# A hybrid decoder layer on one core: the second norm's root is spread by a transposition and two transfers, and DVE's scans, convolutions and a Strassen product stand in another order

## The chip, the cores and the metric

The kernel runs on one core of a Trainium2 chip. Its time is the device time of one execution in microseconds; the median of the runs is given. Engines are named as the profile names them: PE is TensorE, DVE is VectorE, ACT is ScalarE, POOL is GpSimd and SP is SyncE, which here issues transfers only.

## What is computed

One decoder layer over 512 tokens of width 1024, in float32:

```
x = x + 0.5 * swiglu(rmsnorm(x, ffn1_norm), gate, up, down)      # FF 2816
h = rmsnorm(x, mix_norm)
proj = h @ w_in                    # q, k, v, o, gates, pool channels
qk = silu(causal_dwconv(proj[q, k], conv_w, conv_b))             # 4 taps
hm = mlstm_chunkwise(q, k, v, i_pre, f_pre)                      # 4 heads x 128
hm = sigmoid(o) * (hm * rsqrt(mean(hm * hm) + EPS) * mh_norm)
hp = multiscale_pool(proj[pool], pool_w, pool_scale)
x = x + concat(hm, hp) @ w_out
x = x + 0.5 * swiglu(rmsnorm(x, ffn2_norm), gate, up, down)
return rmsnorm(x, final_norm)
```

where `rmsnorm(x, g) = x * rsqrt(mean(x * x) + EPS) * g`, the mean going over the 1024 channels of a token.

## The kernel before, in words

**Layout.** x lies with channels on the 128 partitions and the 512 tokens along the free axis (`x[P, 8, T]`). Every product is made in three passes of reduced-precision matmuls (`three_passes`, L412 to L416): high times high, high times low, low times high. So each weight unit of 128x1024 that SP loads into `raw` (two buffers, L297) is split by ACT into `w_hi` (L845) and by DVE into `w_lo` (L1309); four slots hold split units. The norm's gain goes into x before the product, and the root, one number a token, is multiplied into the product afterwards, by DVE, from `rinv[P, T]`, the same row on every partition.

**Order.** Nothing schedules this program: each engine's list of instructions is written out by hand in its own function, and semaphores join them. The stages are the first FFN (`ffn_up`, `ffn_down`), the mixer, the second FFN and the last norm.

**A norm's root.** While the squares are being summed over partitions, PE makes four columns of means (`mean_columns`, L473, one column for each block of 128 tokens). DVE turns them into roots in ten dependent steps on a [128, 4] tile (`inverse_rms`, L1354, and `rsqrt`, L1339 to L1347), each counted in `col_step`. Then `replicate` (L477) has PE spread them: for each of the four blocks one fp32 matmul of 128x128 with the column broadcast as the stationary operand and the identity as the moving one (L465) gives the row on all partitions of PSUM bank 7. DVE copies that to `rinv` (`take_rinv`, L1363). The kernel does so for the first, second and third norm.

**The mixer's first part.** Units are numbered from MIX. Unit MIX holds the gates. Then come units MIX+1, 2, 3, 4, 6, 7, 9, 10 (`QK_UNIT`, one block of q or k each, 8 k-steps of three matmuls into one of three PSUM banks in turn), MIX+5, 8, 11, 12 (`V_UNIT`), and from MIX+13 (`O_UNIT`) on the output gates and pool channels. PE runs the second norm's means inside the first q/k block (`mean_hook`) and `replicate(1)` right behind that block. From the fourth q/k block on it waits until DVE has read the bank three blocks back (`u_made`).

On DVE, `mixer` begins with the root (`inverse_rms(1)`), `take_rinv(1)`, `gates_in` (the gates' product with rinv at L1629, two small operations, L1631 and L1632) and a split. Then each round of the loop over units reads the block's product, times rinv, into `work` (L1682), runs the three taps of the convolution for the block before (`taps`, L1661), splits a unit, and makes the low half of the finished q/k (`qk_lo`, L1672). `gates_first` and `gates_second` (scans at L1647, L1651, L1653) stand in the rounds of `V_UNIT[0]` and `V_UNIT[1]`. ACT starts the gates' logarithm after DVE's product (L1067 to L1071) and the convolution's first tap (L1089).

**The heads' roots.** Each head's root is spread in another way: PE transposes the [128, 4] columns to 4 rows of 128 (`head_turn`, L691), ACT copies them to `turned` (L1150), SP writes them to DRAM (L381) and, when that has landed, reads them back onto all partitions (`spread_root`, L385), and DVE multiplies by them (L1748).

**The Strassen loops.** All but a few of the 22 gate/up blocks of an FFN are made by a scheme of seven products on halves (`period`, L519 to L521: 84 matmuls of 256 columns, in the order 1, 5, 3 of the iteration before, 6, 4 of the iteration before, 2, 7). The first matmul of a period waits for `prod_made`, DVE's product of silu and up of two iterations before (`product`, L1460 and L1462). DVE's `iteration` holds four sums of weight blocks (L1399, L1407, L1411, L1418), seven low halves (L1426), the gate (L1451, L1454), the product and two corners (L1468, L1474). SP reloads each of the four weight blocks when DVE has used it (L315). Iterations 0 and 1 are written out, the others stand in a loop.

## Time and profile before

| what | value |
|---|---|
| median of 3 runs | 895.78 us (895.74 to 896.03) |
| the profiled execution | 896.22 us, span in the profile 894.4 us |
| PE busy | 887.2 us (99%), 5572 matmuls |
| PE weight loads | 804.4 us (90%) |
| DVE busy | 673.8 us (75%), 1158 instructions |
| ACT busy | 450.1 us (50%) |
| POOL busy | 42.7 us (5%) |
| chain that ended last | PE 95%, DVE 3%, ACT 1% |
| granted clock of PE, mean | 0.998 of full speed |
| DVE busy, 120 to 270 us | 124.41 of 150 us |
| DVE busy, 50 to 120 us | 67.11 of 70 us |
| DVE busy, 360 to 420 us | 44.08 of 60 us |

The span goes from the first to the last instruction; the device time is a little longer. Matmuls overlap and their ends are modelled, so PE's busy time says little of short stalls: the distance between the starts of two matmuls says more. The first Strassen loop lies at about 52 to 227 us, the mixer begins at about 353 us, and the second loop at about 562 us. Line numbers are those of the kernel before.

### The profile page before, as it was taken

How to read it: one execution, taken by the hardware profiler on the slowest of the kernel's cores; microseconds unless marked ns; L12 is line 12 of the kernel's file. 1: busy time of each engine (PE TensorE's matmuls, PEld its weight loads, DVE VectorE, ACT ScalarE, POOL GpSimd, SP SyncE). 2: the span in 40 equal slices, each digit the busy share in tenths (PEclk: the TensorE clock that was granted, in tenths of full speed). 3: DMA queues.
4: the chain of work that ended last, by engine and by line, in shares of the span. 5: the costliest groups of instructions: out<-in, count | busy, mean ns of one | idle time of the engine just before them, and what ended most of it. 6: DMA issues, size and time to landing. Idle time of an engine off the chain costs nothing.

```text
span 894.4 us, 15568 instructions
## 1 busy us (share of the span) xinstructions
PE 887.2 (99%) x5572; PEld 804.4 (90%) x5572; DVE 673.8 (75%) x1158; ACT 450.1 (50%) x753; POOL 42.7 (5%) x63
## 2 busy tenths in 40 slices
PE   9999999999999999999999999999999999999997
PEld 7899999999988888888888888999999999888887
DVE  7999999999553534677886699899999998534334
ACT  7665666666432323444853374666666665323221
POOL 0000000000000000001435100000000000000000
PEclk9999999999999999999999999999999999999999
DMA  6233333332523332223323232333323332433312
GB/s 247 94 116 98 97 112 104 110 94 70 177 104 108 100 111 95 93 72 107 107 72 99 83 125 71 107 106 111 100 95 111 100 114 84 136 113 99 112 48 95
DMA packets 39420, 93.84 MB, mean 105 GB/s; under 512 B 4436, under 2 KB 5092, under 8 KB 39384
## 3 DMA queue, kind: packets, MB, share of 16 engines
q1 hardware_dynamic: 39064, 92.83, 31.7%
q0 software_dynamic: 176, 0.46, 0.2%
q8 instruction: 22, 0.36, 0.2%
q14 instruction: 14, 0.11, 0.0%
q10 hardware_dynamic: 144, 0.08, 0.0%
HBM read 91.24 MB, written 2.11 MB: 104 GB/s over the span
## 4 chain that ended last, share of the span: by engine, by line
PE 95%; DVE 3%; ACT 1%; issue 1%; DMA 0%; DVEq 0%; SPq 0%; ACTq 0%
PE ps L414 16%; PE ps L416 16%; PE ps L415 16%; PE ps L519 14%; PE ps L521 14%; PE ps L520 13%; PE ps L444 1%; PE ps L447 1%; PE ps L450 1%; DVE w_lo L1426 1%; PE ps L465 0%; PE ps L820 0%; PE ps L674 0%; PE ps L682 0%; DMA raw<-weights 0%
## 5 line engine op out<-in xcount | busy, mean ns | idle before, releaser
L1309 DVE TENSOR_TENSOR w_lo<-raw,w_hi 128x1024 fp32r<-128x1024 f32 x83 | 101.6, 1224 | 118.7 <-ACT w_hi L845 112.9
L414 PE MATMUL ps<-act_hi,w_hi 128*128 128x512 f32 (+1 forms) x470 | 178.7, 380 | 0.0
L416 PE MATMUL ps<-act_hi,w_lo 128*128 128x512 f32 (+1 forms) x470 | 178.2, 379 | 0.0
L415 PE MATMUL ps<-act_lo,w_hi 128*128 128x512 f32 (+1 forms) x470 | 178.2, 379 | 0.0
L519 PE MATMUL ps<-xg_hi,w_hi 128*128 128x256 f32 x608 | 174.1, 286 | 0.3 <-DVE work L1462 0.3
L521 PE MATMUL ps<-xg_hi,w_lo 128*128 128x256 f32 x608 | 172.2, 283 | 0.0
L520 PE MATMUL ps<-xg_lo,w_hi 128*128 128x256 f32 x608 | 171.9, 283 | 0.0
L845 ACT ACTIVATE w_hi<-raw 128x1024 fp32r<-128x1024 f32 x75 | 79.0, 1056 | 150.9 <-PE ps L416 146.0
L519 PE MATMUL ps<-xe_hi,w_hi 128*128 128x256 f32 x456 | 128.0, 281 | 0.0
L521 PE MATMUL ps<-xe_hi,w_lo 128*128 128x256 f32 x456 | 127.2, 279 | 0.0
L520 PE MATMUL ps<-xe_lo,w_hi 128*128 128x256 f32 x456 | 127.2, 279 | 0.0
L519 PEld LDWEIGHTS ps<-xg_hi,w_hi 128*128 128x128 f32 x608 | 116.2, 191 | 1.8 <-issue 0.9
L520 PEld LDWEIGHTS ps<-xg_lo,w_hi 128*128 128x128 f32 x608 | 116.1, 191 | 0.1
L521 PEld LDWEIGHTS ps<-xg_hi,w_lo 128*128 128x128 f32 x608 | 116.1, 191 | 0.0
L897 ACT ACTIVATE w_hi<-sums 128x512 fp32r<-128x512 f32 x152 | 94.5, 626 | 21.2 <-DVE sums L1399 15.5
L416 PEld LDWEIGHTS ps<-act_hi,w_lo 128*128 128x128 f32 x470 | 88.4, 188 | 16.8
L415 PEld LDWEIGHTS ps<-act_lo,w_hi 128*128 128x128 f32 x470 | 88.4, 188 | 16.6
L414 PEld LDWEIGHTS ps<-act_hi,w_hi 128*128 128x128 f32 x470 | 88.4, 188 | 16.3
L1426 DVE TENSOR_TENSOR w_lo<-sums,w_hi 128x512 fp32r<-128x512 f32 x152 | 100.9, 683 | 1.3 <-ACT w_hi L897 1.3
L519 PEld LDWEIGHTS ps<-xe_hi,w_hi 128*128 128x128 f32 x456 | 85.9, 188 | 0.1
L520 PEld LDWEIGHTS ps<-xe_lo,w_hi 128*128 128x128 f32 x456 | 85.7, 188 | 0.0
L521 PEld LDWEIGHTS ps<-xe_hi,w_lo 128*128 128x128 f32 x456 | 85.6, 188 | 0.0
(221 smaller groups left out, 1377.9 us busy)
## 6 DMA issues: line engine op xcount, KB each, us to landing
raw<-weights SPq DMA_DIRECT2D x85, 512.0 KB, 3.3
raw<-weights SPq DMA_DIRECT2D x152, 256.0 KB, 2.7
x<-x_t SPq DMA_DIRECT2D x8, 256.0 KB, 6.0
first<-weights SPq DMA_DIRECT2D x8, 256.0 KB, 5.7
work<-neg_rows SPq DMA_DIRECT2D x4, 256.0 KB, 3.2
root<-root_rows SPq DMA_DIRECT2D x4, 256.0 KB, 3.8
out<-sums SPq DMA_DIRECT2D x3, 256.0 KB, 2.1
out<-raw SPq DMA_DIRECT2D x3, 256.0 KB, 2.2
```

What stands on the lines that cost most here:

```text
L414: pe.matmul(acc, hi, m_hi, start=first, stop=False)
L415: pe.matmul(acc, hi, m_lo, start=False, stop=False)
L416: return pe.matmul(acc, lo, m_hi, start=False, stop=last)
L444: pe.matmul(ps[:, n], weight(n, k)[0], plain_x(k, 0), start=k == 0, stop=False)
L447: pe.matmul(ps[:, n], weight(n, k)[1], plain_x(k, 0), start=False, stop=False)
L519: pe.matmul(acc, hi[:, at], m_hi, start=first and k == 0, stop=False, skip_group_check=True)
L520: pe.matmul(acc, hi[:, at], m_lo, start=False, stop=False, skip_group_check=True)
L521: mm = pe.matmul(acc, lo[:, at], m_hi, start=False, stop=k == KH - 1, skip_group_check=True)
L845: act.activation(w_hi[:, k % SLOTS], raw[:, k % RAWS], ACT.Copy).then_inc(hi_made, 1)
L897: act.activation(factor(i, par, p)[0], src, ACT.Copy).then_inc(f_hi[i], 1)
L1309: dve.tensor_tensor(w_lo[:, k % SLOTS], raw[:, k % RAWS], f32(w_hi[:, k % SLOTS]), ALU.subtract).then_inc(lo_made, 1)
L1426: dve.tensor_tensor(lo, src, f32(hi), ALU.subtract).then_inc(f_lo[i], 1)
```

## The change

It does three things.

1. The second norm's root is no longer spread by `replicate(1)` and `take_rinv(1)`. PE transposes the columns once (`turn_norm`), before the last k of the first q/k block instead of behind the block. ACT copies the four rows to `turned` (`turn_norm_out`, ahead of its gate operations), SP writes them to a new DRAM tensor `norm_rows` and reads them back into `rinv` on all partitions (`spread_norm`, between the loads of units MIX+5 and MIX+6). DVE waits for that (`norm_spread`) just before the gates' product. The other norms keep the old way.
2. DVE's order in the mixer: the split of unit MIX+4 comes before the gates' product; `gates_second` comes before the split and the low half of its round; the last q/k block is scaled, and the taps of the one before it are run, before the split of unit MIX+13; the last taps come before the copy of the gate columns, and the last low half before the split of unit MIX+14.
3. In iteration 1 of both Strassen loops DVE makes `product` before `sum_4`.

```diff
@@ SP
+            def spread_norm(i):
+                sp.wait_ge(norm_turned, i + 1)
+                sp.dma_start(norm_rows[i].rearrange("(b p) -> b p", p=P),
+                             (turned, mask)[i][0:TB]).then_inc(norm_out, 16)
+                sp.wait_ge(norm_out, 16 * (i + 1))
+                sp.dma_start(rinv[:], norm_rows[i:i + 1].partition_broadcast(P)).then_inc(norm_in, 16)
...
-            units(DN1 + RAWS, MIX + 15)
+            units(DN1 + RAWS, MIX + 6)
+            spread_norm(0)
+            units(MIX + 6, MIX + 15)
@@ PE
+            def turn_norm(stage):
+                pe.wait_ge(col_step, STEPS * (stage + 1))
+                pe.transpose(ps[0:TB, 7, 0:P], ycol[:], ident[:]).then_inc(rep_made, 1)
...
                 def mean_hook(k):
                     if k == 2:
                         mean_columns(1)
+                    if k == KD - 1:
+                        turn_norm(1)
...
                         column_block(n, n, ps[:, qk_bank[i % 3]], mean_hook if i == 0 else None)
-                        if i == 0:
-                            replicate(1)
@@ ACT
+            def turn_norm_out(i):
+                act.wait_ge(rep_made, i + 2)
+                if i >= 1:
+                    act.wait_ge(root_out, 16 * HEADS)
+                act.activation((turned, mask)[i][0:TB], ps[0:TB, 7, 0:P], ACT.Copy).then_inc(norm_turned, 1)
...
                 act.preload_act_table_set("natural_log_exp_and_others")
+                turn_norm_out(0)
@@ DVE
+            def norm_spread(i):
+                dve.wait_ge(norm_in, 16 * (i + 1))
...
                     if not tail:
                         lo_of(6, s + 1, 1 - par)
+                    if second:
+                        product(s - 1, 1 - par)
+                    if not tail:
                         sum_4(s + 1)
-                    if not head:
+                    if not head and not second:
                         product(s - 1, 1 - par)
...
-                iteration(1, 1)
+                iteration(1, 1, second=True)
...
                 inverse_rms(1)
-                take_rinv(1)
...
+                    split_next()
                     dve.wait_ge(g_sum, 2)
+                    norm_spread(0)
                     dve.tensor_tensor(arena[0:36, 0], arena[0:36, 1], rinv[0:36, :], ALU.mult).then_inc(g_dve, 1)
...
+                def scaled(i):
+                    dve.wait_ge(unit_used, QK_UNIT[i] + 1)
+                    dve.tensor_tensor(work[:, i % 2], ps[:, qk_bank[i % 3]], rinv[:], ALU.mult).then_inc(u_made, 1)
...
                 gates_in()
-                split_next()
                 pending = None
                 for n in range(MIX + 1, V_UNIT[2]):
-                    if n in QK_UNIT:
+                    if n in QK_UNIT and n < QK_UNIT[7]:
                         i = QK_UNIT.index(n)
-                        dve.wait_ge(unit_used, n + 1)
-                        dve.tensor_tensor(work[:, i % 2], ps[:, qk_bank[i % 3]], rinv[:], ALU.mult).then_inc(u_made, 1)
+                        scaled(i)
                     if pending is not None:
                         taps(pending)
+                    if n == V_UNIT[1]:
+                        gates_second()
+                    if n == QK_UNIT[6]:
+                        scaled(7)
+                        taps(6)
                     if n < QK_UNIT[7]:
                         split_next()
                         if pending is not None:
                             qk_lo(pending)
-                    pending = i if n in QK_UNIT else None
+                    pending = i if n in QK_UNIT and n < QK_UNIT[6] else None
                     if n == V_UNIT[0]:
                         gates_first()
-                    if n == V_UNIT[1]:
-                        gates_second()
+                taps(7)
                 dve.wait_ge(cols_made, 1)
                 dve.tensor_copy(cols[:], ps[:, 3, 0:2 * TB * HEADS]).then_inc(cols_made, 1)
-                taps(7)
                 qk_lo(6)
+                qk_lo(7)
                 split_next()
-                qk_lo(7)
```

How the instructions stand in the built programs, at the three places that matter. Line numbers are each program's own.

DVE at the start of the mixer, from the root's last step to the first q/k scaling; before, then changed:

```order
L1347 SCALAR_TENSOR_TENSOR ycol<-bcol,ycol 128x4 [waits col_step]
L1359 COPY rcol<-ycol 128x4 [waits col_step]
L1363 COPY rinv<-ps 128x512 [waits rep_made]
L1625 COPY arena<-ps 36x512 [waits rinv_made]
L1627 TENSOR_TENSOR arena<-ps,arena 36x512 [waits g_sum]
L1629 TENSOR_TENSOR arena<-arena,rinv 36x512 [waits g_sum]
L1631 TENSOR_SCALAR arena<-arena,vec 4x512 [waits g_dve]
L1632 TENSOR_SCALAR arena<-arena,vec 4x512
L1309 TENSOR_TENSOR w_lo<-raw,w_hi 128x1024 [waits hi_made]
L1682 TENSOR_TENSOR work<-ps,rinv 128x512 [waits unit_used]
```

```order
L1373 SCALAR_TENSOR_TENSOR ycol<-bcol,ycol 128x4 [waits col_step]
L1385 COPY rcol<-ycol 128x4 [waits col_step]
L1656 COPY arena<-ps 36x512
L1658 TENSOR_TENSOR arena<-ps,arena 36x512 [waits g_sum]
L1335 TENSOR_TENSOR w_lo<-raw,w_hi 128x1024 [waits hi_made]
L1662 TENSOR_TENSOR arena<-arena,rinv 36x512 [waits norm_in,g_sum]
L1664 TENSOR_SCALAR arena<-arena,vec 4x512 [waits g_dve]
L1665 TENSOR_SCALAR arena<-arena,vec 4x512
L1704 TENSOR_TENSOR work<-ps,rinv 128x512 [waits unit_used]
```

The copy of rinv is gone, the split of unit MIX+4 has moved from behind the gates' operations to ahead of them, and the gates' product now waits for the transfer (`norm_in`).

DVE at the sixth to eighth q/k block (i = 5, 6, 7): from the taps of block 5 to the low halves of blocks 6 and 7; before, then changed:

```order
L1661 SCALAR_TENSOR_TENSOR work<-work,vec 128x509 [waits conv_step]
L1309 TENSOR_TENSOR w_lo<-raw,w_hi 128x1024 [waits hi_made]
L1672 SCALAR_TENSOR_TENSOR act_lo<-work,act_hi 128x512 [waits qk_hi_made]
L1651 SCALAR_TENSOR_TENSOR arena<-arena 4x512
L1652 TENSOR_SCALAR sums<-arena 4x512 [waits g_dve]
L1653 SCALAR_TENSOR_TENSOR arena<-arena 4x512
L1682 TENSOR_TENSOR work<-ps,rinv 128x512 [waits unit_used]
L1309 TENSOR_TENSOR w_lo<-raw,w_hi 128x1024 [waits hi_made]
L1682 TENSOR_TENSOR work<-ps,rinv 128x512 [waits unit_used]
L1661 SCALAR_TENSOR_TENSOR work<-work,vec 128x511 [waits conv0,u_made]
```

```order
L1694 SCALAR_TENSOR_TENSOR work<-work,vec 128x509 [waits conv_step]
L1684 SCALAR_TENSOR_TENSOR arena<-arena 4x512
L1685 TENSOR_SCALAR sums<-arena 4x512 [waits g_dve]
L1686 SCALAR_TENSOR_TENSOR arena<-arena 4x512
L1335 TENSOR_TENSOR w_lo<-raw,w_hi 128x1024 [waits hi_made]
L1709 SCALAR_TENSOR_TENSOR act_lo<-work,act_hi 128x512 [waits qk_hi_made]
L1704 TENSOR_TENSOR work<-ps,rinv 128x512 [waits unit_used] x2
L1694 SCALAR_TENSOR_TENSOR work<-work,vec 128x511 [waits conv0,u_made]
L1694 SCALAR_TENSOR_TENSOR work<-work,vec 128x510 [waits conv_step]
L1694 SCALAR_TENSOR_TENSOR work<-work,vec 128x509 [waits conv_step]
L1335 TENSOR_TENSOR w_lo<-raw,w_hi 128x1024 [waits hi_made]
```

The scans pass a split and a low half; the last split of each piece, that of unit MIX+13, now stands behind both scalings and the three taps.

DVE in iteration 1 of a Strassen loop, around the product; before, then changed:

```order
L1426 TENSOR_TENSOR w_lo<-sums,w_hi 128x512 [waits f_hi6]
L1418 TENSOR_TENSOR sums<-raw,sums 128x512 [waits f_lo3,s2_made,blk_in1]
L1460 TENSOR_TENSOR work<-work 128x256 [waits c22_made,silu_made]
L1462 TENSOR_TENSOR work<-ps,work 128x256 [waits p_done4]
L1426 TENSOR_TENSOR w_lo<-raw,w_hi 128x512 [waits f_hi4]
```

```order
L1455 TENSOR_TENSOR w_lo<-sums,w_hi 128x512 [waits f_hi6]
L1489 TENSOR_TENSOR work<-work 128x256 [waits c22_made,silu_made]
L1491 TENSOR_TENSOR work<-ps,work 128x256 [waits p_done4]
L1447 TENSOR_TENSOR sums<-raw,sums 128x512 [waits f_lo3,s2_made,blk_in1]
L1455 TENSOR_TENSOR w_lo<-raw,w_hi 128x512 [waits f_hi4]
```

The sum has moved behind the two multiplications; what follows keeps its place.

## Rows read from the trace of the kernel before

**Rows 1.** The waits of TensorE: engine, line, waited for, us in total, times, longest.
```profile
PE ps L820 <- DVE sums L1893: 1.2, 1, 1.2
PE ps L519 <- DVE work L1462: 0.3, 1, 0.3
```

**Rows 2.** Timeline, TensorE, second norm's broadcasts: start, us, engine, line, instruction, count.
```profile
363.40 0.39 PE L416 MATMUL ps<-xg_hi,w_lo 128*128 128x512 f32 x1
363.62 1.05 PE L465 MATMUL ps<-ident,ycol 128*128 128x128 f32 x8
...
364.98 0.39 PE L416 MATMUL ps<-xg_hi,w_lo 128*128 128x512 f32 x1
```

**Rows 3.** Timeline, TensorE, a transposition of the same form for head 3.
```profile
476.30 0.39 PE L416 MATMUL ps<-xg_hi,w_lo 128*128 128x512 f32 x1
476.52 0.27 PE L691 MATMUL ps<-ident,ycol 128*4 128x128 f32 x1
...
477.10 0.39 PE L416 MATMUL ps<-xg_hi,w_lo 128*128 128x512 f32 x1
```

**Rows 4.** Timeline, all engines, head 0's root: transposition, second issue, DVE's reader.
```profile
448.35 0.27 PE L691 MATMUL ps<-ident,ycol 128*4 128x128 f32 x1
...
450.12 0.32 SPq L385 DMA_DIRECT2D root<-root_rows  x1
...
454.24 0.69 DVE L1748 TENSOR_TENSOR arena<-arena,root 128x512 f32<-128x512 f32 x1 [0.45 <-DMA root<-root_rows]
```

**Rows 5.** Timeline, DVE in the mixer.
```profile
361.38 0.16 DVE L1347 SCALAR_TENSOR_TENSOR ycol<-bcol,ycol 128x4 f32<-128x4 f32 x1
...
366.88 0.68 DVE L1629 TENSOR_TENSOR arena<-arena,rinv 36x512 f32<-36x512 f32 x1
...
368.51 1.21 DVE L1309 TENSOR_TENSOR w_lo<-raw,w_hi 128x1024 fp32r<-128x1024 f32 x1
369.64 0.67 DVE L1682 TENSOR_TENSOR work<-ps,rinv 128x512 f32<-128x512 f32 x1
...
418.53 1.23 DVE L1309 TENSOR_TENSOR w_lo<-raw,w_hi 128x1024 fp32r<-128x1024 f32 x1 [1.83 <-ACT w_hi L845]
...
420.27 2.73 DVE L1661 SCALAR_TENSOR_TENSOR work<-work,vec 128x511 f32<-128x511 f32 x3
```

**Rows 6.** Timeline, TensorE: first matmuls of units MIX+4 and MIX+13.
```profile
375.43 0.39 PE L414 MATMUL ps<-xg_hi,w_hi 128*128 128x512 f32 x1
...
427.05 0.44 PE L414 MATMUL ps<-xg_hi,w_hi 128*128 128x512 f32 x1
```

**Rows 7.** Timeline, TensorE, first Strassen loop, iterations 1 to 3.
```profile
68.69 0.28 PE L521 MATMUL ps<-xe_hi,w_lo 128*128 128x256 f32 x1
...
69.51 0.28 PE L520 MATMUL ps<-xg_lo,w_hi 128*128 128x256 f32 x1
...
79.28 0.28 PE L521 MATMUL ps<-xe_hi,w_lo 128*128 128x256 f32 x1
79.42 0.38 PE L519 MATMUL ps<-xg_hi,w_hi 128*128 128x256 f32 x1
```

**Rows 8.** Timeline, DVE, the same iterations.
```profile
67.80 0.68 DVE L1418 TENSOR_TENSOR sums<-raw,sums 128x512 f32<-128x512 f32 x1
68.40 0.41 DVE L1460 TENSOR_TENSOR work<-work 128x256 f32<-128x256 f32 x1
...
72.59 0.69 DVE L1399 TENSOR_TENSOR sums<-raw 128x512 f32<-128x512 f32 x1 [0.37 <-DMA raw<-weights]
...
78.87 0.42 DVE L1462 TENSOR_TENSOR work<-ps,work 128x256 f32<-128x256 f32 x1
```

**Rows 9.** Timeline, ACT, the silu of iteration 1.
```profile
66.71 0.63 ACT L901 ACTIVATE work<-work 128x512 f32<-128x512 f32 x1 [1.07 <-DVE work L1454]
```

**Rows 10.** Waits of all engines, one row.
```profile
DVE sums L1399 <- DMA raw<-weights: 8.7, 32, 0.8
```

**Rows 11.** DMA issues by line: engine, count, KB each, median us to landing.
```profile
x<-x_t SPq DMA_DIRECT2D x8, 256.0 KB, 6.0
```

More of the change, by code:

```diff
@@ L105, with build_layer @@
 S_COLS = 1280
-def build_layer(nc, weights, pool_w, x_t, vecs, consts, neg_rows, root_rows, out):
+def build_layer(nc, weights, pool_w, x_t, vecs, consts, neg_rows, root_rows, norm_rows, out):
     ctx = ExitStack()
@@ L239, in build_layer @@
         half_made, qsq_made = sem("half_made"), sem("qsq_made")
+        norm_turned, norm_out, norm_in = sem("norm_turned"), sem("norm_out"), sem("norm_in")
         turn_made, root_out, root_in = sem("turn_made"), sem("root_out"), [sem(f"root_in{i}") for i in range(2)]
@@ L551, in period @@
                     if head:
-                        pe.wait_ge(rinv_made, stage + 1)
+                        pe.wait_ge(rinv_made, 1 + p)
                     else:
@@ L1149, in turn_out @@
                         act.wait_ge(root_out, 16 * h)
+                    else:
+                        act.wait_ge(norm_out, 16)
                     act.activation(turned[0:TB], ps[0:TB, 7, 0:P], ACT.Copy).then_inc(turn_made, 1)
@@ L1363, in take_rinv @@
                 dve.tensor_copy(rinv[:], ps_rep).then_inc(rinv_made, 1)
-                dve.wait_ge(rinv_made, stage + 1)
+                dve.wait_ge(rinv_made, 1 + stage // 2)
             def terms(p, k):
@@ L1474, in corner_22, with iteration @@
                     dve.tensor_tensor(u_half[1], ps_b[par], p5_sb[par], ALU.add).then_inc(c22_made, 1)
-                def iteration(s, par, head=False, tail=False):
+                def iteration(s, par, head=False, tail=False, second=False):
                     if not tail:
@@ L1992 @@
     root_rows = nc.dram_tensor("root_rows", (HEADS, T), F32, kind="Internal").ap()
-    build_layer(nc, *args, neg_rows, root_rows, out)
+    norm_rows = nc.dram_tensor("norm_rows", (2, T), F32, kind="Internal").ap()
+    build_layer(nc, *args, neg_rows, root_rows, norm_rows, out)
     r = run_bass_kernel_spmd(nc, [arrays], core_ids=[0])
```

## The prediction

> **What bounds the kernel now.** I read the waits of TensorE first, since a change to a vector-side detail is worth what it takes out of the engine that sets the end. The profile lists three, of which two count: 1.2 us at the very start and 0.3 us before L519 on DVE's L1462 [rows 1]. So the time is TensorE's own instruction stream, and I weigh it by the distance between starts of matmuls (the ends are modelled). Then come the stretches that the change touches: TensorE around the four broadcasts of the second norm [rows 2] and around an isolated transposition of the same form [rows 3], the existing pair of root transfers [rows 4], DVE and TensorE in the mixer [rows 5, 6], and the two engines in the Strassen loop [rows 7, 8]. The reader is to see that in the mixer TensorE waits for nobody, while in the loop DVE is just as full as TensorE.
>
> **Part 1, the second norm.** Four fp32 matmuls of L465 go, one transposition comes.
> - Removed: L416 starts at 363.40, the four broadcasts follow, and the third matmul behind them (L416) starts at 364.98: 1.58 us for three steps [rows 2]. A step of this stream is 0.227 us: from this L416 to the first matmul of the fourth q/k block at 375.43 are 46 steps and 10.45 us [rows 2, 6], and three steps are 0.68. Cost 1.58 - 0.68 = 0.90 us.
> - Added: the same reading around head 3's transposition: 476.30 to 477.10 is 0.80 us for three steps [rows 3], so it costs 0.80 - 0.68 = 0.12 us.
> - Net: 0.90 - 0.12 = 0.78 us less TensorE time, on the path, since nothing in the mixer holds TensorE back.
>
> By its duration in the row the transposition is 0.27 us [rows 3], and that is the other bound of its cost; I take 0.12, because the path pays the distance between starts and the end of a matmul is only modelled. The Trainium skill (TensorE: Matmul & The Clock Gate, Part 4) gives about 275 ns for one in a kernel's context; by that figure the estimate of the saving would be 0.62 us in place of 0.78. The duration of the row agrees with it, the distance between starts does not.
>
> Does the transposition wait? It stands before the last k of its block, two steps before 363.40, so at 362.94. DVE's last step of the root starts at 361.38 and takes 0.16 [rows 5]. It is ready 1.4 us earlier: no wait.
>
> What it starts is longer than before: copy on ACT, a 2 KB transfer out, a 256 KB broadcast in. Head 0's root does just this: transposition at 448.35, second issue at 450.12, DVE's reader at 454.24, 5.89 us in all [rows 4]. From 362.94 that gives 368.8 for DVE's gate product (L1629), which ran at 366.88 [rows 5]. From L1629 to the next split are 1.63 us (366.88 to 368.51) and the first scaling (L1682) takes 0.67 [rows 5], so that scaling ends at 368.8 + 1.6 + 0.7 = 371.1, 0.8 us later than before. DVE fills the wait: the copy of rinv is gone, and the 1.2 us split of unit MIX+4, 368.51 before, comes ahead of it. Who waits? TensorE's fourth q/k block (unit MIX+4) needs this scaling for its bank. It began at 375.43 [rows 6] and would now begin at 374.65. Cover: 3.5 us. Behind the waiting DVE product stand the scaling and the split of unit MIX+5, and that unit is not read before the block after, 5.4 us later. ACT's three gate operations move by the same 2 us and are ahead of nothing that TensorE needs sooner. On SP the load of unit MIX+6 now stands behind both transfers, but it could never start before the split of MIX+4, which was at 368.51: with the split moved ahead it starts earlier, not later. Cost 0.
>
> **Part 2, scans, convolutions, splits in the mixer.** Same instructions, other order. The scans and the row of negatives come sooner, by at least the split and the low half that they pass: TensorE was not waiting for them, gain 0. The one thing made later is the split of unit MIX+13: it ran at 418.53 and now stands behind a scaling (0.7) and the three taps (2.7) [rows 5], so by the worst count it starts at 421.9 and ends at 423.2. TensorE reads it at 427.05, or 426.3 after the saving [rows 6]. Cost 0; without that 3 us cover it would be a direct stall.
>
> **Part 3, the first product in each Strassen loop.** In iteration 1 the two multiplications L1460 and L1462 now precede the sum L1418, which takes DVE 0.60 us (67.80 to 68.40) [rows 8]. In the first FFN this is where the 0.3 us wait of [rows 1] sits: from 68.69 to the second start behind it, 69.51, are 0.82 us, where two steps of 0.119 (69.51 to 79.28, 82 steps) would be 0.24 [rows 7]. So 0.58 us are lost, and L1462 0.60 us sooner would remove nearly all of it. Nothing stops the swap: ACT's silu started at 66.71 and takes 0.63 [rows 9], so it is done before DVE would reach L1460 at 67.80 [rows 8]; and the TensorE product that L1462 reads is the fifth of the seven of a period, the seventh being under way by then.
>
> But is it kept? TensorE's next period starts at 79.42 [rows 7], again just behind L1462 (78.87 + 0.42 = 79.29) [rows 8]. Between the two DVE is idle once, 0.37 us at 72.59, for a transfer [rows 8], and that transfer is released by DVE's own L1426 behind the product, which keeps its time: the swap only permutes three instructions in front of it. The same idle, and no other, stands in the later iterations: 32 waits, 8.7 us [rows 10]. So DVE's chain runs on its own clock, TensorE would arrive at 79.42 - 0.58, wait, and go on at 79.42. Bounds: 0 and 0.58 us; I take 0, since 79.42 is fixed by DVE. In the second FFN [rows 1] shows no such wait, and 0 is the only value.
>
> **Sum.** -0.78 + 0 + 0 = -0.78 us. The profiled execution took 896.22 us (span 894.4) and would take 895.44; it lay 0.44 above the median of the three runs, 895.78, so the median becomes **895.0 us**. That is 0.09%, and a measurement of this kernel tells about 0.2% (1.8 us) from no change.
>
> **Rivals.**
> - *The product's gain is kept too.* For it: the wait is real and is removed. Against: the start at 79.42 is again 0.13 us behind L1462. It gives 895.78 - 0.78 - 0.58 = 894.4.
> - *The saved matmuls are given back.* TensorE, 0.78 us ahead, would then run into something that keeps its time, as in part 3. In the mixer no wait is listed [rows 1], and the second loop starts from work that TensorE itself releases, so it moves along. It gives 895.8.
> - *The transfers come late (the slower side).* The only known pair lands in time, but a transfer in a full queue can take 6.0 us, as those of x at the start do [rows 11]. If both took that, the gate product would begin 12.0 us behind the transposition and more, in place of 5.9 [rows 4], so 6.1 later; the cover is 3.5, and TensorE would stand still for 2.6 us before the fourth q/k block: 895.0 + 2.6 = 897.6. It decides from 3.5 us of delay. Against: the queue holds no other load there, since MIX+5 was issued before and MIX+6 comes behind.
> - *More than the sum.* Some wait within DVE's chain shortens in every iteration. It would need over 1.8 us in total; nothing in the rows says so. 893.8 or less.
>
> **Numbers.** Forecast 0.76; product's gain kept 0.10; given back 0.06; transfers late 0.04; more than the sum 0.04. The range runs from 894.2 (the kept gain, less 0.2 for the spread of runs) to 896.0 (given back, with the same spread). Faster by over 0.2%: 0.04, and 0.01 for errors of mine in the same direction, 0.05. Slower by over 0.2%: the late transfers, 0.05 with the same. Within: 0.90.
>
> **What would show it.** One transposition before the last k of the first q/k block and no stall around it; three steps across it of about 0.80 us; DVE's gate product at about 368.8 and idle before it, put down to a transfer; TensorE without a wait at the fourth q/k block; L1460 in the first loop at 67.8 in place of 68.40, TensorE's period there starting at 68.8, and the next one still at 79.4 with a listed wait where there was none. If the next one starts at 78.9, part 3 is wrong. If TensorE shows a wait on L1682's scaling, part 1 is. A time outside 894.2 to 896.0 means a mechanism that I have not seen.

## The result and the profile after

The changed kernel takes **897.35 us** (median of 21 runs, 896.11 to 898.46) against 895.92 us (21 runs, 894.97 to 896.59) for the kernel before beside it: a ratio of 1.0016, 95% interval 1.0010 to 1.0022. The forecast was 895.0 us in a range of 894.2 to 896.0: the change loses 1.4 us (0.9 to 2.0 by the interval) where 0.8 were to be gained. The profiled execution took 897.64 us (span 895.8), 1.42 us more than the one of before, so the loss is in the trace.

First the timeline of all engines around the second norm, the part of the change that was to gain (columns as in [rows 2]; weight loads and the plain matmuls in between left out):

```profile
363.05 0.27 PE L496 MATMUL ps<-ident,ycol 128*4 128x128 f32 x1
363.19 1.21 DVE L1335 TENSOR_TENSOR w_lo<-raw,w_hi 128x1024 fp32r<-128x1024 f32 x1
363.36 0.27 ACT L1076 ACTIVATE turned<-ps 4x128 f32<-4x128 f32 x1 [3.41 <-PE ps L496]
363.65 0.33 SPq L356 DMA_DIRECT2D norm_rows<-turned  x1
364.84 0.35 SPq L359 DMA_DIRECT2D rinv<-norm_rows  x1
365.54 0.34 SPq L298 DMA_DIRECT2D raw<-weights  x1
368.94 0.68 DVE L1662 TENSOR_TENSOR arena<-arena,rinv 36x512 f32<-36x512 f32 x1 [4.54 <-DMA rinv<-norm_rows]
```

All as forecast. The transposition waits for nothing, the split of MIX+4 fills DVE's wait, and the gates' product starts at 368.94 (forecast 368.8, [rows 5] 366.88). Two of the matmuls around it:

```profile
362.82 0.39 PE L427 MATMUL ps<-xg_hi,w_lo 128*128 128x512 f32 x1
...
363.62 0.39 PE L427 MATMUL ps<-xg_hi,w_lo 128*128 128x512 f32 x1
```

Three steps across the transposition take 0.80 us, where the four broadcasts made them 1.58 [rows 2]: 0.78 us are saved. So where does 1.42 come from? I set milestones on TensorE side by side: the first of the mean's matmuls in each stage, and the first and last matmul of each Strassen loop.

| stretch on TensorE | before | after |
|---|---|---|
| first loop, first to last matmul | 182.01 us | 182.79 us |
| mixer, second norm's mean to third norm's mean | 358.61 to 545.04 | 358.71 to 544.94 |
| second loop, first to last matmul | 561.86 to 762.95 (201.09) | 561.78 to 764.37 (202.59) |

The first loop began 0.68 us earlier and ended at the same time (233.53, 233.63). The mixer is 0.2 us shorter; its 0.78 are there, but 0.6 of them are lost again at head 0. The **second loop is 1.50 us longer**, and that is the loss. No part of the change touches that loop by more than one permutation in its second iteration. TensorE's first matmul of it and DVE at its head, of before:

```profile
561.86 0.28 PE L519 MATMUL ps<-xg_hi,w_hi 128*128 128x256 f32 x1
...
563.51 0.69 DVE L1432 TENSOR_TENSOR act_lo<-work,act_hi 128x512 fp32r<-128x512 f32 x1 [0.70 <-ACT act_hi L906]
564.21 0.69 DVE L1399 TENSOR_TENSOR sums<-raw 128x512 f32<-128x512 f32 x1
```

and of after:

```profile
561.78 0.28 PE L535 MATMUL ps<-xg_hi,w_hi 128*128 128x256 f32 x1
...
563.43 0.69 DVE L1461 TENSOR_TENSOR act_lo<-work,act_hi 128x512 fp32r<-128x512 f32 x1 [0.70 <-ACT act_hi L922]
565.07 0.69 DVE L1428 TENSOR_TENSOR sums<-raw 128x512 f32<-128x512 f32 x1 [0.95 <-DMA raw<-weights]
```

DVE's first sum over weight blocks starts 0.86 us later (3.29 us behind TensorE's first matmul of the loop, and not 2.35), for a transfer that it did not wait for before. SP issued it at the same place (561.50 before, 561.42 after). What is in its way shows in the DMA queues of two stretches. Before, 560.4 to 561.4 us, ahead of the blocks:

```profile
q8 instruction: 1, 0.02, 5.9%
```

Before, 562.1 to 564.7 us, while the blocks come:

```profile
q1 hardware_dynamic: 288, 0.52, 62.4%
issues: line engine op xcount, KB each, median us to landing
raw<-weights SPq DMA_DIRECT2D x1, 256.0 KB, 3.0
```

After, the same 562.1 to 564.7 us (560.4 to 561.4 has no packet):

```profile
q1 hardware_dynamic: 282, 0.51, 63.0%
q8 instruction: 1, 0.02, 2.8%
issues: line engine op xcount, KB each, median us to landing
raw<-weights SPq DMA_DIRECT2D x1, 256.0 KB, 3.7
```

None comes while a Strassen loop repeats, from 82 to 236 us and from 591 to 770 us. Whose program it is, the distance between two of them tells. Busy time in a stretch of before, from one such packet to the next (378.4 and 407.1 us):

```profile
378.40:407.10 28.70, 28.70 (x128) 23.79 (x127) 23.40 (x31) 13.08 (x17) 0.00 (x0) 1.00 0.29 92
```

The row counts 128 matmuls and 127 weight loads that lie in the stretch or reach into it. In the trace, 126 of each and 4 semaphore waits of TensorE start between the two packets: 256 instructions, 64 bytes each, so this is TensorE's program. From the packet at 351.2 us to the one at 560.5 us the count is 2,045, or 256 for each of eight. The four broadcasts were 8 matmuls (x8 in [rows 2]) and 8 loads; the transposition is one and one. So from the second norm on, TensorE's program is 14 instructions shorter, and a load of it should come 14 x 0.113 = 1.6 us of work later (0.113 is half of the 0.227 us step). Here it does: 562.15 - 560.5 = 1.65. Not every load follows: of the eight from 378 to 562 us, five came 0.9 to 1.7 us later, two 0.1 to 0.2 us earlier and one 1.9 us earlier, and why is not shown. The one at 562.15 meets the first blocks of the second loop, whose packets begin at 562.4.

The rest is spread over the loop. DVE's first sum of iterations 3 and 19, before and after:

```profile
581.52 0.69 DVE L1399 TENSOR_TENSOR sums<-raw 128x512 f32<-128x512 f32 x1 [0.26 <-DMA raw<-weights]
743.26 0.69 DVE L1399 TENSOR_TENSOR sums<-raw 128x512 f32<-128x512 f32 x1 [0.27 <-DMA raw<-weights]
```

```profile
582.43 0.69 DVE L1428 TENSOR_TENSOR sums<-raw 128x512 f32<-128x512 f32 x1 [0.30 <-DMA raw<-weights]
744.69 0.69 DVE L1428 TENSOR_TENSOR sums<-raw 128x512 f32<-128x512 f32 x1 [0.31 <-DMA raw<-weights]
```

161.74 and 162.26 us for 16 iterations, 10.109 and 10.141 each: 0.03 us in each, 0.57 over the 17 from the second sum (571.50 and 572.36) to the last. 0.86 + 0.57 = 1.43 us is what DVE's last sum is late by, and behind the loop the two executions take the same time (131.5 us). The waits of all engines say the same in one row ([rows 10] had 8.7, 32, 0.8):

```profile
DVE sums L1428 <- DMA raw<-weights: 10.8, 34, 0.9
```

### The profile page after: what moved, and what is told of

Same layout as the page of the kernel before. It is cut to its first block, busy times and chain, and to the rows that moved or that the text cites. A ratio compares the mean times of both kernels' runs of the same rounds, so it can differ in the third digit from the quotient of the medians.

```text
span 895.8 us, 15559 instructions
## 1 busy us (share of the span) xinstructions
PE 887.8 (99%) x5565; PEld 803.7 (90%) x5565; DVE 675.0 (75%) x1157; ACT 449.3 (50%) x754; POOL 45.3 (5%) x63
## 4 chain that ended last, share of the span: by engine, by line
PE 84%; DVE 8%; ACT 3%; issue 2%; DMA 2%; POOL 1%; DVEq 0%; SPq 0%; ACTq 0%
PE ps L425 14%; PE ps L535 13%; PE ps L426 13%; PE ps L427 13%; PE ps L537 13%; PE ps L536 13%; DVE work L1694 2%; DMA raw<-weights 1%; DVE w_lo L1455 1%; PE ps L455 1%; PE ps L461 1%; PE ps L458 1%; DVE w_lo L1335 1%; ACT w_hi L861 1%; DVE work L1704 0%
```

## Which part of the change it is

Four kernels, each the kernel before with one or two parts of the change. The product of iteration 1 moved ahead of the sum (`iteration(1, 1, second=True)`, in both Strassen loops), and nothing else:

> The kernel before with nothing but iteration 1's product ahead of sum_4 in both Strassen loops. Theory A (the swap is neutral: TensorE's first period starts 0.6 us earlier, the next one is held by DVE's chain): within 0.3 us of before, L1462 0.6 us earlier and TensorE's start of the period after next unchanged. Theory B (the swap disturbs DVE's chain, and the second loop pays for it, where the changed kernel's trace shows TensorE 1.5 us longer in the loop): 1 to 1.5 us slower than before, and the second loop longer than the 201.1 us of before.

The norm part: the transposition, its copy, the two transfers and the split ahead of the gates' product; scans, convolutions and loops as before (`gates_in()` now holds the `split_next()` that stood behind it):

> The kernel before with only the second norm's transposition, its two transfers and the split of unit MIX+4 ahead of the gates' product; scans, convolutions and both loops as before. Theory A (the saving of 0.78 us is real and only this part has it): 0.6 to 0.9 us faster than before, no wait of TensorE at head 0's mean. Theory B (something that comes with this part, its transfers or its longer queue program, lengthens the loops): as slow as the changed kernel or between, with the saving of 0.78 us visible inside the mixer all the same.

The order of scans, convolutions and late splits alone:

> The kernel before with only the scans, convolutions and late splits of the mixer in the changed order. Theory A (POOL's key sums of head 0 start earlier, fall on DVE's two splits of 128x1024, slow down, and hold ACT and then TensorE at head 0's mean): a wait of TensorE of 0.3 to 0.5 us at head 0's mean, POOL's second key-sum instruction over 2 us in place of 1.0, 0.4 to 0.7 us slower than before. Theory B (that wait comes from the norm's later gates, not from the order): no such wait, within 0.2 us of before.

Norm and order together, that is the change without the product:

```diff
-                iteration(1, 1, second=True)
+                iteration(1, 1)
```

> The changed kernel without the swap in the loops. If the swap is what makes the changed kernel slower: 0.8 us slower to 0.3 us faster than before (0.78 saved, 0.6 lost at head 0's mean), at least 1 us faster than the changed kernel's 1.4 us over before. If the swap is neutral: as slow as the changed kernel, 1.4 us over before.

| kernel | median, us | ratio to before (interval) | mixer, mean to mean | second loop |
|---|---|---|---|---|
| product alone | 896.23 | 1.0002 (0.9993 to 1.0011) | 186.40 | 201.12 |
| norm alone | 898.95 | 1.0033 (1.0021 to 1.0045) | 187.60 | 202.99 |
| order alone | 895.79 | 0.9999 (0.9990 to 1.0008) | 186.40 | 200.83 |
| norm and order | 897.42 | 1.0017 (1.0008 to 1.0026) | 185.58 | 202.43 |

The product and the order are worth nothing alone. The norm part has the loss, and its second loop is as long wherever it is in. With the order, the mixer of the profiled execution gains 0.85 us (186.43 before, 185.58); without it, TensorE waits once for DVE's scores. From the waits of the norm-alone kernel:

```profile
PE ps L425 <- DVE arena L1742: 1.4, 1, 1.4
```

So the order is what covers the norm's later root, worth 1.5 us of median beside it (898.95 to 897.42) and 2.0 us of the mixer. My expectation that the order alone would cause head 0's stall was a miss: it appears in neither kernel with the order, though once in the kernel after:

```profile
440.59 0.80 PE L698 MATMUL ps<-vec,arena 128*128 128x1 f32 x6 [0.42 <-ACT dcol L1167]
```

There POOL's first key sum of head 0 took 2.31 us beside DVE's splits and 1.01 us in the kernel with norm and order. Of the four profiled executions with the change's order in the mixer and nothing added to TensorE there (this one, norm and order, and two of the kernels below), the other three have POOL's sum at 1.0 us and a mixer of 185.58 to 185.63 us, against 186.23 here. So I count it as scatter. It also means that the profiled execution of the kernel after has 0.6 us which most executions need not have, while its difference from before (1.42) is that of the medians (1.43). The profiled execution of norm and order took only 0.76 us more than that of before, with medians 1.7 us apart. Single traces of these kernels don't settle their medians to better than about 1 us.

## Is it the program load, or the transfers?

Three kernels. The kernel after with four tiny matmuls, which put 16 instructions back into TensorE's program, in front of a wait in the first loop's head:

```diff
...
+                    if head and p == 0:
+                        for _ in range(4):
+                            pe.matmul(ps_a[0:32, 0:1], ident[0:32, 0:32], ident[0:32, 0:1], start=True, stop=True)
                     product(2, s, par, ps_a, True)
```

> The kernel after, with four matmuls of 32 x 32 weights and one column added on TensorE in the first loop's head, in front of a wait that it has there (0.43 us). They do no work that anything reads; they add 8 matmuls and 8 weight loads, 16 instructions, about what the four broadcasts had more than the transposition (16 against 2). Theory A (the time is lost since TensorE's program, which comes in packets of 16,384 bytes, one for each 256 instructions, is now loaded 14 instructions later: at 562.15 us, on the block loads of the second loop's head, and not at 560.5): that packet is back before 561.0 and done before the blocks' first packet, DVE's first sum of the second loop starts at 564.2 to 564.4 after TensorE's first matmul there plus 2.35 (before; 3.29 in the kernel after), and the median is 0.8 to 1.5 us below the kernel after's 897.35: 895.9 to 896.6. Theory B (it is the two added transfers and their tensor, by whatever they do to the later loads): the median stays at 897.2 to 897.6 and DVE's wait for raw<-weights at 10.5 us or more over the execution. Theory C (both, the packet for the head and the transfers for the 0.03 us in each iteration): 896.4 to 896.8, the head as under A, the iterations still at 10.13 to 10.14 us.

The reverse in the kernel before, a program 12 instructions shorter:

```diff
-            for _ in range(WARMUPS):
-                pe.matmul(ps_rep[:, 0:HALF], zeros[:, 0:P], zeros[:, 0:HALF], start=True, stop=True)
-            pe.matmul(ps_rep[:, 0:P], zeros[:, 0:P], zeros[:, 0:P], start=True, stop=True)
+            for _ in range(2):
+                pe.matmul(ps_rep[:], zeros[:, 0:P], zeros[:, 0:1].broadcast_to([P, T]), start=True, stop=True)
```

> The kernel before, with its five warm-up matmuls of 256 and 128 columns made as two of 512 columns: 12 instructions fewer on TensorE (its program loads come about 12 x 0.113 = 1.4 us of work later), 128 columns fewer, all else as it was. Theory A: the packet of 560.5 comes at 561.6 to 562.0, and so still works when the block loads of the second loop's head begin (562.4); DVE's first sum there starts 0.3 to 0.9 us late and the median is 0.4 to 1.4 us above the kernel before's: 896.1 to 897.2. Theory B: no norm part is in it, the time stays within 0.3 us of the kernel before, the second loop at 200.8 to 201.2 us.

And the transfers alone in the kernel before (here and below, the declarations of the new tensor and semaphores are left out of the diffs):

```diff
-            units(DN1 + RAWS, MIX + 15)
+            units(DN1 + RAWS, MIX + 6)
+            sp.dma_start(norm_rows[0].rearrange("(b p) -> b p", p=P), ident[0:TB]).then_inc(norm_out, 16)
+            sp.wait_ge(norm_out, 16)
+            sp.dma_start(root[:, 0], norm_rows[0:1].partition_broadcast(P)).then_inc(norm_in, 16)
+            units(MIX + 6, MIX + 15)
+            sp.wait_ge(norm_in, 16)
```

> The kernel before with the change's two transfers and their tensor alone, at the change's place in the queue of loads (constants written to the new tensor and read back, spread over 128 partitions, into a tile that is idle then); TensorE's program, and the broadcasts of the second norm, as before. Theory A: the program load stays at 560.5, the time within 0.3 us of the kernel before, the second loop at 200.8 to 201.2 us. Theory B: the second loop takes 202.4 to 203.0 us and the median is 1.2 to 1.9 us above the kernel before. Theory C: the head as before, the iterations at 10.13 to 10.14 us, 0.4 to 0.6 us above the kernel before.

The three fit Theory C, both causes. With the small matmuls the packet is at 560.8, DVE's first sum 564.44 - 562.10 = 2.34 us behind TensorE's first matmul (forecast 2.35), and the median is 896.56 us (1.0009, 0.9999 to 1.0018); the iterations stay at 10.145. The shortened program gave the kernel before the loss at the head: the packet at 561.6, 897.06 us, 1.0013 (1.0004 to 1.0022), and in DVE's timeline there (TensorE's first matmul at 560.99) the same wait as in the kernel after:

```profile
564.24 0.69 DVE L1398 TENSOR_TENSOR sums<-raw 128x512 f32<-128x512 f32 x1 [0.91 <-DMA raw<-weights]
```

In that kernel the next load fell on blocks too (579.3 us, where it was 576.6 before), and DVE's third sum waited 0.68 us in place of 0.26. The transfers alone left the head as it was (packet at 560.8, first sum 2.41 us behind TensorE), made the iterations 10.144 us, and cost more than the 0.4 to 0.6 us expected: 897.80 us, 1.0021 (1.0012 to 1.0030). Some 0.3 us of it are in the mixer (186.73 from mean to mean); its profiled execution, at 897.38, lies 0.4 below its median, and that part I can't place.

The four small matmuls had an accident of their own: they moved the first loop's load from 82.0 to 81.3 us as well, and one iteration there took 11.12 us. The next kernel has them in the mixer instead (at the head of `head_mean(0)`, into an idle bank). 

```diff
                 def head_mean(h):
+                    if h == 0:
+                        for _ in range(4):
+                            pe.matmul(ps[0:32, 7, 0:1], ident[0:32, 0:32], ident[0:32, 0:1], start=True, stop=True)
```

> The kernel after with the four small matmuls (16 instructions, 0.34 us of TensorE in the run that had them in the first loop's head) in the mixer instead, ahead of head 0's mean, so that the first loop's program loads stay where they were: there, one had moved from 82.0 to 81.3 us and one iteration had taken 11.12 us. Theory A: the first loop as in the kernel after (182.8 us), the program load of the second loop's head at 560.6 to 561.4, DVE's first sum there 2.35 us after TensorE's first matmul and not 3.29, and a median of 896.1 to 896.7 us: 0.86 us better at the head, 0.34 us worse where the matmuls stand, less what they hide in head 0's wait. If only the first loop's accident was what those matmuls cost, it is below the 896.56 us of that run by 0.2 to 0.5 us. Against Theory A speaks a time at 897.2 or more with the load at 561 or before.

With it went three parts of the transfers' kernel. Its write alone (the second `dma_start` and the last wait taken out):

> The kernel before with the first of the change's two transfers alone (4 rows of 128 to the new tensor, in packets of 512 bytes that only 4 of the 16 DMA engines carry), at the change's place, and the loads' loop split there as the change splits it; constants are written and nothing reads them. The kernel with both transfers was at 897.80 us with the second loop's iterations at 10.144 us and, there, 0.43 us from the last packet of a block to DVE's sum, against 10.08 to 10.11 us and 0.38 us without them. Theory C1 (the write to 4 engines only does it, since it leaves the 16 engines' rings out of step for all that comes later): 897.2 to 898.0 us, 10.13 to 10.15 us, 0.43 us. Theory C2 (the spread to 128 partitions does it): 895.5 to 896.0 us, 10.08 to 10.11 us, 0.38 us.

Its spread alone:

```diff
+            units(DN1 + RAWS, MIX + 6)
+            sp.dma_start(root[:, 0], x_t[0:1].partition_broadcast(P)).then_inc(norm_in, 16)
+            units(MIX + 6, MIX + 15)
+            sp.wait_ge(norm_in, 16)
```

> The kernel before with the second of the two transfers alone (one row read for 128 partitions, here a row of the input, into an idle tile), the loads' loop split there as in the change. Theory C1: 895.5 to 896.0 us, iterations of the second loop 10.08 to 10.11 us. Theory C2: 897.2 to 898.0 us, 10.13 to 10.15 us. If neither of the two runs is slow, or both are, it is something that they share: the split loop in SP's program, or any wait there (Theory D).

And the split loop alone:

```diff
-            units(DN1 + RAWS, MIX + 15)
+            units(DN1 + RAWS, MIX + 6)
+            units(MIX + 6, MIX + 15)
```

> The kernel before, with nothing but the loads' loop of SP split in two at the change's place: the same 15 loads in the same order, no transfer added, 8 rows more in SP's program, which every later row of it is moved by. Theory D (where SP's later program lies, not what it transfers, makes the second loop's iterations longer): 896.8 to 898.0 us, 10.13 to 10.15 us. Theories C1 and C2: as the kernel before, 895.5 to 896.0 us, 10.08 to 10.11 us.

The small matmuls (0.34 us, at 439.41) gave 896.27 us, packet at 559.6, first sum 2.40 us behind TensorE: the head is as in the kernel before. All profiled executions together, those of the kernels below included, say so of the head (times are from TensorE's first matmul of the second loop):

| TensorE's program, against before | kernels | program load | DVE's first sum |
|---|---|---|---|
| as long, or 2 longer | 13 | -1.40 to -1.16 us | 2.28 to 2.50 us |
| 6 shorter | 1 | -0.64 us | 2.26 us |
| 12 shorter | 1 | +0.61 us | 3.25 us |
| 14 shorter | 4 | +0.31 to +0.43 us | 2.94 to 3.59 us |

Of the three kernels with a part of the transfers, **only the spread** to 128 partitions has the long iterations (10.136 us, against 10.105 for the write and 10.081 for the split). That is Theory C2's mark; C1 and D fall. C2's time was wrong: 896.47 us (1.0009, 1.0000 to 1.0018) and not 897.2 to 898.0, against 895.97 (write) and 895.76 (split), with 895.46 before. By the medians alone the three could not be told apart.

## What about a spread transfer lengthens a loop 200 us later?

The packet records give more than the sums' starts: in each iteration, the end of the last packet before DVE's sum, and the sum (iterations in which a packet of another transfer ends in between are left out; the median is taken). In the first loop the two are 0.38 us apart in every kernel; in the second, 0.38 without the spread and 0.43 with it. The packets themselves take no longer. Four more kernels. Two and three spreads in the kernel before; the diff goes from the kernel with one spread to that with three, and the kernel with two fills `root[:, 0]` and `root[:, 1]` from rows 0 and 1 of `x_t`:

```diff
-            sp.dma_start(root[:, 0], x_t[0:1].partition_broadcast(P)).then_inc(norm_in, 16)
+            for tile in (root[:, 0], root[:, 1], t1_odd[:]):
+                sp.dma_start(tile, x_t[0:1].partition_broadcast(P)).then_inc(norm_in, 16)
             units(MIX + 6, MIX + 15)
-            sp.wait_ge(norm_in, 16)
+            sp.wait_ge(norm_in, 48)
```

> The kernel before with two transfers of one row to 128 partitions at the change's place (one alone gave 896.47 us, iterations of 10.136 us in the second loop and 0.43 us from a block's last packet to DVE's sum; none 895.46 us, 10.08 to 10.11 us and 0.38 us). Theory P (it is whether the number of such transfers before the loop is odd or even, so that each block's packets meet another place of the rings): 895.4 to 896.0 us, 10.08 to 10.11 us, 0.38 us. Theory Q (such a transfer costs what it costs each time, or its presence does it): 896.3 to 897.5 us, 10.13 us or more, 0.43 us or more.

> The kernel before with three such transfers there. Theory P: as with one, 896.2 to 896.8 us, iterations of 10.13 to 10.15 us, 0.43 us from last packet to sum. Theory Q: 896.5 us or more, and more than with two. A step of another length (four, or eight transfers) would show as two and three both slow, or both as before.

The kernel after with one more spread, with the small matmuls in the mixer and without:

```diff
             spread_norm(0)
+            sp.dma_start(root[:, 0], norm_rows[0:1].partition_broadcast(P)).then_inc(even_in, 16)
             units(MIX + 6, MIX + 15)
+            sp.wait_ge(even_in, 16)
```

> The kernel after with the four small matmuls in the mixer (alone 896.27 us) and one more spread of the norm's row, into an idle tile, right behind the norm's own. Theory P: the second loop's iterations back to 10.08 to 10.11 us, 0.5 to 0.7 us less than with the small matmuls alone: 895.5 to 895.9 us, and the second loop at 200.7 to 201.2 us; against the kernel before, -0.2 to +0.3 us (the transposition's 0.8 us gained, less 0.34 us of small matmuls and what the mixer's stalls take). Theory Q: 896.2 us or more.

> The kernel after with the one more spread alone, the program load left on the block loads at the second loop's head. Theory P: 896.6 to 896.9 us (897.35 less 0.5 to 0.7 us), iterations at 10.08 to 10.11 us, DVE's first sum still 3.2 to 3.4 us after TensorE's first matmul of the loop. Theory Q: 897.2 us or more.

And, since neither odd nor mere presence fitted, five of them (the last two into the first two tiles again, each behind a wait for all before it); and, beside it, the kernel after with one more spread and `range(2)` in place of `range(4)` for the small matmuls:

> The kernel before with five transfers of one row to 128 partitions at the change's place; their waits hold back loads there, so that the time as a whole says little, and the second loop is what is read. Theory P4 (what counts is the number of such transfers modulo four): as with one, iterations of the second loop 10.12 to 10.15 us, 0.43 us from a block's last packet to DVE's sum. Theory R (one is a case by itself, or the step is another): 10.08 to 10.11 us, 0.38 us.

> The kernel after with the one more spread and two of the small matmuls (8 instructions, 0.17 us) in place of four (896.03 us). Theory A: 8 instructions move the program load forward by 8 x 0.113 = 0.9 us of work, to 0.5 us before TensorE's first matmul of the second loop; it takes 0.9 to 1.4 us and the blocks' packets begin 0.6 us after that matmul, so it is done or nearly done: first sum 2.35 to 2.7 us after the first matmul, and 895.7 to 896.2 us.

| added spreads | kernel | iteration, us | last packet to sum | median, us (before beside it) |
|---|---|---|---|---|
| 0 | before | 10.109 | 0.38 | 895.92 |
| 0 | before, split loop | 10.081 | 0.38 | 895.76 (895.46) |
| 0 | before, write | 10.105 | 0.38 | 895.97 (895.46) |
| 1 | before, spread | 10.136 | 0.43 | 896.47 (895.46) |
| 1 | before, both transfers | 10.144 | 0.43 | 897.80 (895.71) |
| 1 | after | 10.141 | 0.43 | 897.35 (895.92) |
| 1 | after, four small matmuls in the first loop | 10.145 | 0.43 | 896.56 (895.71) |
| 1 | after, four small matmuls in the mixer | 10.121 | 0.43 | 896.27 (895.46) |
| 2 | before | 10.082 | 0.38 | 896.72 (895.90) |
| 3 | before | 10.101 | 0.38 | 896.04 (895.90) |
| 5 | before | 10.141 | 0.43 | 897.28 (896.25) |
| 2 | after | 10.084 | 0.38 | 896.25 (895.90) |
| 2 | after, four small matmuls | 10.099 | 0.38 | 896.03 (895.90) |
| 2 | after, two small matmuls | 10.094 | 0.38 | 896.05 (896.25) |

The sharp sign is the fourth column. In the profiled executions of all 19 kernels it has two values and nothing between: 0.38 us in eleven, 0.43 us in eight. The iterations scatter by 0.03 us among kernels of the same kind, but the kinds don't overlap: 10.081 to 10.113 us (mean 10.095) and 10.121 to 10.145 us (mean 10.137), so the step is worth about 0.04 us in each iteration, 0.7 us in the 17. Most single medians could not show it: their intervals are 0.8 us to either side.

One and five are slow; none, two and three are not: what counts fits the number of full transfers **modulo four**. Theory P, odd against even, fell with three; Theory P4's forecast for five, 10.12 to 10.15 us, was made before that run. Four spreads were not tried.
```profile
582.20 0.69 DVE L1407 TENSOR_TENSOR sums<-raw 128x512 f32<-128x512 f32 x1 [0.39 <-DMA raw<-weights]
744.46 0.69 DVE L1407 TENSOR_TENSOR sums<-raw 128x512 f32<-128x512 f32 x1 [0.26 <-DMA raw<-weights]
```

```profile
581.45 0.69 DVE L1434 TENSOR_TENSOR sums<-raw 128x512 f32<-128x512 f32 x1 [0.29 <-DMA raw<-weights]
743.03 0.69 DVE L1434 TENSOR_TENSOR sums<-raw 128x512 f32<-128x512 f32 x1 [0.36 <-DMA raw<-weights]
```

162.26 against 161.58 us for the 16 iterations. Two spreads in the kernel before, at 896.72, are no contradiction: its second loop is 200.76 us, and the loss is in the mixer (187.25 us from mean to mean). It is the stall of head 0 again, in a kernel without the change's order:

```profile
441.76 1.02 PE L687 MATMUL ps<-vec,arena 128*128 128x1 f32 x8 [0.62 <-ACT dcol L1148]
```

The number of transfers is not its cause, since with three and five of them the mixer is 186.42 and 186.43 us, as before.

With both causes undone the kernel after has a second loop of 200.91 us and is back at 896.03 us, 0.9999 (0.9990 to 1.0008); with half of the small matmuls 896.05, 1.0000 (0.9991 to 1.0009), packet at 560.6. With the extra spread alone it was 896.25, better than the 896.6 to 896.9 expected: there the packet took 0.90 us, DVE waited 0.60, and its first sum was 2.94 us behind TensorE. So with the iterations put right, the load at the head is worth 0.2 us by the medians (896.25 to 896.03), less than their intervals can tell. None of the three beats the kernel before by what can be measured. In the traces the mixer with four small matmuls is 186.13 us, 0.30 us less than before, and 0.50 us more than without them (185.63): of the transposition's gain they leave 0.3 us, and 0.8 us to either side is what the interval allows.

## Why the prediction was wrong

- **Part 1, price and place: right.** Saved 0.78 us as forecast, no wait at the transposition, product at 368.94 against 368.8, no wait at the fourth q/k block. The reading of distances between starts was the right one here.
- **Part 1, "Cost 0": incomplete.** The cover held, but only with part 2 beside it. The norm alone makes TensorE wait 1.4 us, much further on, for head 0's scores. I followed the delayed product to the next q/k blocks and not along the gates' chain.
- **Part 2, gain 0:** right alone (895.79), wrong beside part 1 (1.5 us of median). I costed edits one by one whose worth is in the pair.
- **Part 3: right.** L1489 started at 67.55 and L1491 at 67.88, TensorE's wait there went and another came where none was: its next period began at 79.14 behind L1491 at 78.59. That is 0.3 us before the forecast 79.42, and the first loop ended where it had (233.53, 233.63).
- **The step that failed** is in the rival on saved time given back: "the second loop starts from work that TensorE itself releases, so it moves along." The loop starts from DVE's sum over blocks, and that from a transfer; TensorE's program load moved the other way, onto that transfer, and DVE's chain, which I had rightly found to be the clock of the first loop, kept the 0.86 us to the end. In the kernel before, TensorE had no gap in the second loop until 669 us, since DVE began with a lead; in the kernel after the first is at 567.39 us.
- **What the sum lacked** is two terms: the program load on the blocks, +0.94 us at the loop's head (3.29 - 2.35), and one more spread transfer, +0.57. The profiled execution adds up with them: +0.1 up to the mixer, -0.78 + 0.6 in it, +0.94 + 0.57 in the second loop are +1.43, for a measured +1.42. That the medians differ by as much is in part luck, since head 0's 0.6 us stands in one of four such executions; without it the terms give +0.8, and the rest of the medians' 1.43 us (0.9 to 2.0) is not traced.
- **The chances.** 0.05 for slower rested on one mechanism, late transfers, which did not come. The range had nothing for the loop's four loads in an iteration, on which a DVE wait of 8.7 us [rows 10] already hung: I read that row as constant because DVE's own work was.

## What to carry to other kernels

Where an engine's chain waits a little for a transfer in every iteration, any change upstream that shifts the DMA queues can be paid for there, 200 us later: price it from that wait, not from zero. TensorE's instructions are loads too: taking instructions out of its program moves later program loads, and the place to look at is the one where a queue runs empty and refills (a loop's head). And edits that move one chain belong together in the sum, since one can be the other's cover.

## What the runs showed of the hardware

- TensorE's program comes in packets of 16,384 bytes, one for each 256 instructions (126 matmuls, 126 weight loads and 4 waits between two) outside the repeating loops, each 0.9 to 1.7 us on one DMA engine. One on top of two 256 KB transfers made the second land 3.7 and not 3.0 us after its issue, and DVE's dependent sum 0.86 us late. The Trainium skill (DMA: Bandwidth & Descriptors, Queues, rings and completion order) says that an engine drains a whole packet of one queue row before it goes to another; a landing 0.7 us late would fit it, but no run here shows it, since the rows don't name the engine.
- Against TensorE's first matmul of the loop the load with 14 instructions fewer came 1.7 us later (computed 1.6), with 12 fewer 2.0 (1.4), with 16 more again 1.7 earlier (1.8), and DVE's first sum followed each way.
- The time from a block's last packet to the DVE instruction that waits for it was 0.38 us, and 0.43 us when one or five more transfers of 144 packets (128 of 2,048 bytes, 16 of 4) stood ahead of the loop; with none, two or three it was 0.38. A transfer of 8 packets (4 of 512 bytes, 4 of 4) did not count.
- An fp32 matmul of 32 x 32 weights and one column is two matmuls and two weight loads, and four such (x8 in the profile) took 0.34 us.
